# Weights as host-packed blocks with one contiguous 16 KB row per partition, and four token tiles loaded behind the third weight block

## The reference, cut to what matters

```
h = rms_norm(x, norm_mix);  z = h @ w_in
q, kc, vc, ksl, vsl, kw, vw, g, u = split(z)
x = x + concat(sparse_attention(q, kc, vc, ksl, vsl, kw, vw, g),   # compressed, selected, window branches
               conformer_conv(u)) @ w_out
x = x + memory_cross_attention(rms_norm(x), rms_norm(mem), w_mq, w_mk, w_mv, w_mo)
x = x + (silu(h3 @ w_gate) * (h3 @ w_up)) @ w_down,  h3 = rms_norm(x)
```

## Time and profile before

| | |
|---|---|
| median of 3 runs | 1902.3 us (1901.12 to 1903.95) |
| profiled execution | 1897.38 us, span of the slowest core (core 7) 1896.3 us |
| spans of the 8 cores | 1884.6 to 1896.3 us |
| PE busy | 1730.8 us, 91% of the span |
| DVE, ACT, POOL busy | 756.5, 534.7, 160.2 us |
| POOL's DMA queue (software_dynamic) | 182,224 packets, 111.32 MB, 46.3% of 16 engines |
| SP's DMA queue (hardware_dynamic) | 22,640 packets, 52.93 MB, 8.8% |

### The profile page before, as it was taken

The page is one execution under the profiler, slowest core; times in us unless marked ns, Lnnn a source line. Parts: engine busy times, 40 slices in busy tenths (PEclk is TensorE's granted clock), DMA queues, the critical chain, the costliest instruction groups (busy, mean ns, idle before and its releaser), DMA issues.

```text
span 1896.3 us, 30031 instructions; the slowest of 8 cores (1884.6 to 1896.3 us)
## 1 busy us (share of the span) xinstructions
PE 1730.8 (91%) x10862; PEld 939.1 (50%) x10862; DVE 756.5 (40%) x1521; ACT 534.7 (28%) x920; POOL 160.2 (8%) x150
## 2 busy tenths in 40 slices
PE   2699998999996668997789999999999999999998
PEld 1456645666663326865444444444444444444444
DVE  3343122566575454342652332515233251523325
ACT  2243244778676544122551000000000000000000
POOL 2000100000001231001000001000010100001000
PEclk9899999999998988998999999999999999999999
DMA  9920887234136439659317439093663919366364
GB/s 253 164 89 1 95 84 96 49 51 73 35 47 128 122 73 217 95 67 138 44 24 111 64 45 124 14 129 43 92 86 49 125 14 128 42 92 87 48 89 178
DMA packets 205007, 166.17 MB, mean 88 GB/s; under 512 B 14400, under 2 KB 194240, under 8 KB 200512
## 3 DMA queue, kind: packets, MB, share of 16 engines
q0 software_dynamic: 182224, 111.32, 46.3%
q1 hardware_dynamic: 22640, 52.93, 8.8%
HBM read 258.18 MB, written 8.52 MB: 141 GB/s over the span
## 4 chain that ended last, share of the span: by engine, by line
PE 79%; DMA 7%; DVE 4%; ACT 4%; another core or an unknown queue 3%; issue 2%; POOL 1%; SPq 1%; DVEq 0%; ACTq 0%; POOLq 0%
PE bank L1428 16%; PE pair L1425 15%; PE pair L1508 8%; PE bank L1508 8%; PE pair L564 4%; DMA arena<-sel 4%; PE bank L564 4%; PE bank L1266 3%; PE pair L870 2%; PE bank L849 2%; PE bank L723 2%; PE bank L718 2%; PE pair L1319 2%; PE pair L1266 1%
## 5 line engine op out<-in xcount | busy, mean ns | idle before, releaser
L1428 PE MATMUL bank<-arena 128*128 128x512 bf16 x1408 | 318.7, 379 | 0.0
L1425 PE MATMUL pair<-arena 128*128 128x512 bf16 x1344 | 303.8, 379 | 0.0
L1431 ACT ACTIVATE arena<-pair 128x512 bf16<-128x512 f32 x84 | 50.1, 597 | 806.4 <-PE pair L1425 806.4
L1432 DVE TENSOR_TENSOR arena<-bank,arena 128x512 bf16<-128x512 f32 x88 | 60.8, 691 | 537.9 <-PE pair L1425 411.0
L859 ACT ACTIVATE arena<-bank,arena 128x512 bf16<-128x512 f32 (+3 forms) x402 | 215.4, 574 | 75.7 <-PE pair L870 30.9
L1428 PEld LDWEIGHTS bank<-arena 128*128 128x128 bf16 x1408 | 137.6, 98 | 165.4
L1425 PEld LDWEIGHTS pair<-arena 128*128 128x128 bf16 x1344 | 131.6, 98 | 158.5
L1508 PE MATMUL bank<-arena 128*128 128x512 bf16 x704 | 166.3, 379 | 0.0
L1508 PE MATMUL pair<-arena 128*128 128x512 bf16 x704 | 166.3, 379 | 0.0
L870 PE MATMUL pair<-arena 128*128 128x129 bf16 (+1 forms) x1184 | 125.3, 226 | 18.4 <-DVE arena L863 14.7
L1511 DVE TENSOR_TENSOR arena<-pair,arena 128x512 f32<-128x512 f32 x176 | 121.6, 691 | 34.1 <-DVE arena L1511 20.6
(11 more groups left out here) (184 smaller groups left out, 1657.4 us busy)
## 6 DMA issues: line engine op xcount, KB each, us to landing
arena<-xc SPq DMA_DIRECT2D x24, 1024.0 KB, 10.7
arena<-w_gate POOLq DMA_DIRECT2D x22, 1024.0 KB, 14.2
arena<-w_up POOLq DMA_DIRECT2D x22, 1024.0 KB, 15.9
arena<-w_down POOLq DMA_DIRECT2D x22, 1024.0 KB, 12.5
arena<-w_in POOLq DMA_DIRECT2D x18, 1024.0 KB, 13.6
arena<-w_out POOLq DMA_DIRECT2D x10, 1024.0 KB, 18.4
arena<-arena SPq DMA_DIRECT2D x64, 135.0 KB, 2.5
y<-arena SPq DMA_DIRECT2D x8, 1024.0 KB, 3.9
```

Of the source, the lines that this page charges most:

```text
L1425: op(PE, lambda: nc.tensor.matmul(bank[pg][:, :], lhsT=wgt[:, kc, cc * 128:(cc + 1) * 128], rhs=hb[:, kc, :], start=(kc == 0), stop=(kc == ...
L1428: op(PE, lambda: nc.tensor.matmul(bank[pu][:, :], lhsT=wut[:, kc, cc * 128:(cc + 1) * 128], rhs=hb[:, kc, :], start=(kc == 0), stop=(kc == ...
L1432: op(DVE, lambda: nc.vector.tensor_tensor(out=actT[aj][cc][:, tc * 512:(tc + 1) * 512], in0=bank[pu][:, :], in1=sgt[sj][:, :], op=ALU.mult ...
```

## The change

The host packs every weight block into one array, `wblk`, block after block, each as 128 partition rows of 4096 float32 (16 KB); blocks that the ring loads twice are stored once. The device loads block `at` of it into a slot with the same shape as before; the ring's order is the old one. At the start the number of blocks that may be issued is held in `wlimit`: block 0 behind x1, blocks 1 to 3 behind x2, 4 and 5 behind x7. SP waits for block 2's landing before it loads x4, and so x4 to x7. norm_a of tile 4 moves from ahead of the first projection into the middle of the first block, and everything of tiles 4 to 7 moves back by one place, so that norm_b(7) and norm_a(8) stand behind group 0. w_g, w2k and w2v are issued after group 1.

```
-        def wissue(upto=None, behind=None):
+        self.wlimit = 0
+
+        def wissue(limit=None, behind=None):
             POOL.wait(behind)
-            while self.wnext_issue < (len(self.wq) if upto is None else upto):
+            if limit is not None:
+                self.wlimit = limit
+            while self.wnext_issue < self.wlimit:
...
-                dma(POOL, dst, src, w=[wslotb[s_]])
+                dma(POOL, dst, self.wblk_d[at, :, :].rearrange("p (k n) -> p k n", k=shp[0]), w=[wslotb[s_]])
...
         wissue(1, xtok[1])
-        wissue(2, xtok[3])
-        wissue()
-        dma(POOL, wg[:, :, :], self.w_g.rearrange("(k p) n -> p k n", p=128), w=[wgb])
-        dma(POOL, w2[:, 0, :], self.w2k, w=[w2b])
-        dma(POOL, w2[:, 1, :], self.w2v, pw=[w2b])
-
+        wissue(4, xtok[2])
...
             norm_tile_a(xt[xj][:, :], [xtb[xj]], xs0[j], xs0b[j], ss0[j], ss0b[j])
+            if gt == 0:
+                SP.wait(list(wslotb[2].w.values())[0])
             if gt + NX < 16:
-                xload(gt + NX)
+                xtok.append(xload(gt + NX))
+            if gt == 3:
+                wissue(6, xtok[7])
...
+        def late_loads():
+            dma(POOL, wg[:, :, :], self.w_g.rearrange("(k p) n -> p k n", p=128), w=[wgb])
+            dma(POOL, w2[:, 0, :], self.w2k, w=[w2b])
+            dma(POOL, w2[:, 1, :], self.w2v, pw=[w2b])
+
         norm_a(0)
         for gt in range(4):
-            norm_a(gt + 1)
+            if gt < 3:
+                norm_a(gt + 1)
             norm_b(gt)
...
         def next_norm(q_, k_):
-            if q_ < 3 and k_ < 4:
-                gt = (q_ + 1) * 4 + k_
+            gt = (q_ + 1) * 4 + k_
+            if q_ == 0 and k_ < 4:
+                if k_ > 0:
+                    norm_b(gt - 1)
+                norm_a(gt)
+            elif q_ < 3 and k_ < 4:
                 norm_b(gt)
                 if gt + 1 < 16:
                     norm_a(gt + 1)
...
+            if q_ == 0:
+                norm_b(7)
+                norm_a(8)
+                wissue(len(self.wq))
+            if q_ == 1:
+                late_loads()
...
+        out[k] = b.transpose(1, 0, 2).reshape(128, 4096)
```

More of the change, by code:

```diff
@@ L44 @@
 NPTS = 7
+KV_COLS = {"kc": C_KC, "vc": C_VC, "ksl": C_KSL, "vsl": C_VSL, "kw": C_KW, "vw": C_VW}
+BLOCK_ORDER = list(KV_COLS) + [f"q{i}" for i in range(4)] + ["w1k", "w1v"]
+for _i in range(4):
+    BLOCK_ORDER += [f"ua{_i}", f"ub{_i}"]
+BLOCK_ORDER += ["mk0", "mk1", "mv0", "mv1"] + [f"wo{i}" for i in range(8)] + ["mq0", "mq1", "wo1", "wo0", "mq0", "mq1", "mo0", "mo1"]
+BLOCK_ORDER += ["gt0", "up0", "gt1", "up1", "dn0", "dn1"]
+for _i in range(2, 22):
+    BLOCK_ORDER += [f"gt{_i}", f"up{_i}", f"dn{_i}"]
+BLOCKS = list(dict.fromkeys(BLOCK_ORDER))
+BLOCK_AT = {n: i for i, n in enumerate(BLOCKS)}
+NBLK = len(BLOCKS)
 class Sem:
@@ L312, in build @@
         self.memb = dr("memb", [256, D])
-        self.w_in = dr("w_in", [D, IN_W])
         self.w_g = dr("w_g", [D, 24])
[L315 to L324, removed]
+        self.wblk_d = dr("wblk", [NBLK, 128, 4096])
         self.w2k = dr("w2k", [128, 128])
@@ L408, in wissue @@
                     break
-                src, shp = self.wq[i]
+                at, shp = self.wq[i]
                 s_ = i % NSLOT
                 dst = wslot[s_][:, :].rearrange("p (k n) -> p k n", k=shp[0])
-                dma(POOL, dst, src, w=[wslotb[s_]])
+                dma(POOL, dst, self.wblk_d[at, :, :].rearrange("p (k n) -> p k n", k=shp[0]), w=[wslotb[s_]])
                 self.wnext_issue += 1
@@ L448, in wdone @@
             wissue()
[L450 to L488, removed]
+        kvblocks = ["kc", "vc", "ksl", "vsl", "kw", "vw"]
+        for name in BLOCK_ORDER:
+            self.wq.append((BLOCK_AT[name], (32, 128) if name[:2] == "w1" else (2, 2048) if name[:2] in ("mo", "dn") else (16, 256)))
+        self.wo_at = BLOCK_ORDER.index("wo0")
         wg = self.tile(G, "wg", [128, 16, 24], BF16)
@@ L611, in build, with kv_block @@
         kvw = []
-        def kv_block(q_, c0, kind, k_, mid):
+        def kv_block(q_, kind, k_, mid):
             t0_, hb_ = 32 + (q_ % 2) * 512, hTb[q_ % 2]
@@ L656, in build @@
         for q_ in range(4):
-            for k_, (c0, kind) in enumerate(kvblocks):
+            for k_, kind in enumerate(kvblocks):
                 if q_ > 0 or kind not in ("kw", "vw"):
-                    kv_block(q_, c0, kind, k_, lambda: next_norm(q_, k_))
+                    kv_block(q_, kind, k_, lambda: next_norm(q_, k_))
+            if q_ == 0:
[4 more added lines that the diff above has]
+                late_loads()
         S0.close()
@@ L1589, in _pvec, with _pack_blocks @@
     return pv
+def _pack_blocks(I):
+    f = lambda n: np.asarray(I[n], np.float32)[0]
+    w_in, w_out = f("w_in"), f("w_out")[np.concatenate([np.arange(1024), 1024 + CPERM])]
+    cols = lambda w, c: w[:, c:c + 256].reshape(16, 128, 256)
+    rows = lambda w, r: w[r:r + 256].reshape(2, 128, 2048)
+    out = np.empty((NBLK, 128, 4096), np.float32)
+    for n, k in BLOCK_AT.items():
+        if n in KV_COLS:
+            b = cols(w_in, KV_COLS[n])
+        elif n[:2] == "w1":
+            b = f("cmp_k_w1" if n == "w1k" else "cmp_v_w1").reshape(32, 128, 128)
+        else:
+            kind, i = (n[:-1], int(n[-1])) if n[0] == "q" else (n[:2], int(n[2:]))
+            if kind == "q":
+                b = cols(w_in, C_Q + 256 * i)
+            elif kind in ("ua", "ub"):
+                b = cols(w_in, C_U + 256 * i + (1024 if kind == "ub" else 0))
+            elif kind in ("mo", "dn"):
+                b = rows(f({"mo": "w_mo", "dn": "w_down"}[kind]), 256 * i)
+            elif kind == "wo":
+                b = cols(w_out, 256 * i)
+            else:
+                b = cols(f({"mk": "w_mk", "mv": "w_mv", "mq": "w_mq", "gt": "w_gate", "up": "w_up"}[kind]), 256 * i)
+        out[k] = b.transpose(1, 0, 2).reshape(128, 4096)
+    return out
 def make_in_maps(I):
@@ L1596, in make_in_maps @@
     shared = {
[L1597 to L1600, removed]
+        "w_g": np.ascontiguousarray(w_in[:, C_G:C_G + 24]), "wblk": _pack_blocks(I),
+        "w2k": f(I["cmp_k_w2"])[0], "w2v": f(I["cmp_v_w2"])[0],
         "pvec": _pvec(I),
```

## The result

The changed kernel takes 1871.44 us (median of 4 runs, 1871.28 to 1876.15), the kernel before, beside it, 1901.71 (median of 4, 1894.23 to 1903.95). The ratio is 0.9854 with an interval of 0.9822 to 0.9885, so 22 to 34 us less. The forecast was 1874, with 1867 to 1881 for the likeliest case. In the profiled executions the slowest core's span falls from 1896.3 to 1869.9 (26.4), the mean of the eight cores from 1889.5 to 1868.0 (21.5). Some executions run with the cores of one die at a lower granted clock and take some per cent longer; times, ratios and traces here are of the others, and of pieces_4k, which had no other, only the undisturbed die is read.

What follows compares the result with a forecast made beforehand. PE was taken as the bound, with 79% of the chain, and its stops at the start as the main gain. Start 21.2, w_mo 5 and biasT 2 sum to 28.2 us, taking the median from 1902.3 to 1874, range 1857 to 1891.

Steps and rivals of the forecast that it cites:

- the tail before the second group: End of the first projection group: norm_b(7), 8 transposes and two DVE passes hold PE for 3.8 us.
- a stop at x4 in the middle of vc: First projection group: PE stalls 7 us for token tile 4, replacing the old stops.
- block 2 lands at 36: Start: weight blocks land at 24, 30 and 36 us, so SP issues x4 at 36.
- The start: Up to the second projection group: it begins at 75.8 us instead of 96.98, a gain of 21.2 us.
- the bound I named for the forecast: Start: the forecast is wrong if the second projection group begins before 70 or after 82 us.
- the second rival: Weight stream no faster, 8.9 us a block: second group at 84.8, start gains 12 us, 1890 in all; chance 0.2.
- w_mo: PE's waits for the two w_mo blocks: 6 us instead of 10.7, a gain of 5 us, bounds 0 and 12.
- at 5.9 us each: Weight blocks in the new layout: each takes 5.9 us, w_down's 176 GB/s; bounds 8.9 and 4.2 us.
- biasT: ACT's wait for the biasT load, which shares engines with w_in blocks: gain of 2 us, bounds 0 and 5.
- a sign of being wrong: Between 100 and 860 us: a stretch changing length by more than 3 us other than at biasT.
- Weights faster, no stall: First rival: weights at 250 GB/s, PE runs through x4, second group at 66.8, 1858 in all; chance 0.2.
- SP's wait for block 2 turns against it: Third rival: kernel slower; to lose 4 us block 2 must land after 68 us; chance 0.04.

Runs made afterwards that it cites:

- pieces_4k: The changed kernel with each row of a weight block padded into four pieces (4 KB read, 2 KB written); second projection group at 83.14 us on core 0.
- no_wait: The changed kernel without SP's wait for a block before x4; ratio to the kernel before 0.9799 (0.975 to 0.9848).
- after_again: The changed kernel, unaltered, run once more on another chip; ratio to the kernel before 0.9871 (0.985 to 0.9893).
- order_alone: The kernel before with the new order at the start but the old weight layout; ratio to the kernel before 0.992 (0.9893 to 0.9946).
- pieces_short: The changed kernel with block rows padded so pieces can't merge (1 KB read, 512 B written); ratio to the kernel before 0.9907 (0.9881 to 0.9932).
- late_alone: The kernel before with only w_g, w2k and w2v issued later, after group 1; 1891.8 and 1886.1 us, the kernel before on that chip 1899 to 1907.

## Why the prediction was right in the total and wrong in its parts

**What held.** The pieces are merged: 17,616 packets against 17,600 forecast. PE's first projection is at 29.55 (28.7). The memsets no longer wait, the tail before the second group is 3.23 us (3.8 with the norm's passes), and a stop at x4 in the middle of vc takes the place of the old ones. The stretch from 1000 us on has no new wait. The lone rate of a block was sized right: 176 GB/s taken from w_down, 172 measured, though in the FFN short pieces come near it too (163).

**Step that failed: block 2 lands at 36.** It let SP go at 39.87. Two queue rows of the changed kernel, from 20 to 28 us (to be read against the earlier trace rows):

```profile
q0 software_dynamic: 170, 1.26, 91.0%
q1 hardware_dynamic: 77, 0.18, 11.7%
```

Weights flow at 158 GB/s here, above the 133 that I gave them beside x3 and cbf. 0.32 MB had come before 20 us and 1.38 follow until 36, so 2.96 MB at 36 us, where three blocks are 3.15; the queue passes that at 37.3, 1.3 us late. The rest lies in how a block ends. I had put its last byte, counted over the queue, and SP's release on one moment. Two stretches of the changed kernel, from 35.5 to 37.3 and from 37.3 to 39.5 us; the packets under 512 B are the 16 closing packets of block 2:

```profile
DMA packets 40, 0.28 MB, mean 155 GB/s; under 512 B 6, under 2 KB 6, under 8 KB 6
...
DMA packets 56, 0.38 MB, mean 171 GB/s; under 512 B 10, under 2 KB 10, under 8 KB 10
```

Only six of the 16 had come when as many bytes as three blocks hold were through. They run from 35.90 to 39.31, and SP issues 0.6 us after the last: the engines end a block up to 3.4 us apart (2.1 to 3.4 on the eight cores), and those that are through go on with block 3, of which 0.48 MB (3.63 less 3.15) had moved by 40 us. Blocks 0 and 1 were late in the same way, with their last closing packets at 26.2 and 32.3 where I had 24 and 30. The mis-sized term is thus the landing: a block is not there when its bytes, counted over all engines, are through, but when the slowest engine is. x4 then took 8.9 us to its use instead of 8.2, since it shares its way with block 3. Of the 5.5 us by which the second group missed 75.8, 4.7 are these; 0.8 come after x4 (28.3 us from the norm to the second group instead of 27.5).

What x and cast weights do together shows best in no_wait, queues from 28 to 36 us:

```profile
q0 software_dynamic: 115, 0.89, 62.8%
q1 hardware_dynamic: 115, 0.84, 35.6%
```

The packets are equal in number, as the earlier trace rows had it and as the Trainium skill says ("DMA: Bandwidth & Descriptors", Queues, rings and completion order: an engine goes round its queues packet by packet). The page counts several descriptors to a packet, while a packet of these rows is one row or piece; equal counts over 8 us do not tell after how many of them an engine turns. The sum is 1.73 MB in 8 us, 216 GB/s, where I had 266 for the two: a packet of cast weights takes more of an engine's time than an x packet of the same bytes written, 62.8% against 35.6%.

**The start, then, was forecast at 21.2 and gave 15.7** on the slowest cores (96.98 to 81.26), 16.8 by the mark of the start. It stays inside the bound I named for the forecast (second group between 70 and 82), but only just, and after_again, at 82.26, does not. order_alone and pieces_short are what the second rival (stream no faster) looks like: 86.56 and 83.90, against the 84.8 it named, though with lone streams of 139 and 134 GB/s (means of the cores) and not 118.

**w_mo: forecast 5, measured 1 to 2.** The waits are 9.64 us together instead of 6 (10.73 before). The step that failed is "at 5.9 us each". Counted from the issue of the first of the four blocks (862.63 before, 839.75 after), I had them in at 8.0, 15.1, 20.9 and 26.9 us; by their last closing packets they were in at 9.1, 16.9, 23.9 and 30.1, against 9.8, 18.5, 25.0 and 31.6 before. Queue rows of the kernel before, from 872 to 878 us (the second w_mq block, 512 B written a piece) and from 884 to 890 (w_mo, 4 KB):

```profile
q0 software_dynamic: 1547, 0.79, 117.6%
...
q0 software_dynamic: 263, 1.01, 101.7%
```

and of the changed kernel, from 849 to 855 us (the second w_mq block, 8 KB) and from 857 to 863 (w_mo, 8 KB):

```profile
q0 software_dynamic: 117, 0.96, 95.7%
...
q0 software_dynamic: 134, 0.98, 102.5%
```

w_mq went from 132 to 160 GB/s. w_mo, whose pieces were long already, did not gain: 168 before, 163 after. So two of the four blocks could not get shorter, as the lower bound of the forecast had said, and the other two gained less than 118 against 176 had promised: the data of the lone w_in block came mostly from 288 to 296 us, at 131 GB/s, and 118 is what a stretch of 9 us with a start and an end in it gives. Across kernels the stretch with w_mo takes 51.8 to 53.3 us with short pieces (before, order_alone, late_alone, pieces_short) and 48.9 to 50.2 with long ones (the other eight): 2 to 3 us is what length gives there.

**biasT: forecast 2, measured 0.** ACT's wait in the changed kernel, from the view of waits between 280 and 340 us, is 5.6 us against 5.36:

```profile
ACT arena L838 <- DMA arena<-biasT: 5.6, 1, 5.6
```

The lower end of its bounds, 0, was the right one. Why it isn't shorter was not tried.

**Where the total came from.** Sized by the marks: start 16.8, w_mo 2.2, attention and output projection 2.5 (not told from nothing), together 21.5 for the mean core, where 28.2 was forecast. The slowest core's span fell by 26.4: it was 6.8 us above the mean of the eight before and is 1.9 above it after (10.3 in after_again). The median of the runs fell by 30.3, since the profiled execution lay under the median before (1897.4 to 1901.7) and on it after (1871.3 to 1871.4). The slowest core is another one in each profile (7 before, 6 after). From the one to the other POOL's timeline shows 16.9 us at the mark of the start (201.61 to 184.72), 21.1 at the fourth mask of the attention (591.66 to 570.57), 22.9 at the first w_mq block (862.63 to 839.75) and 26.6 at the gate block after w_mo (930.21 to 903.59): 6 us come between the start and w_mq, where I forecast only biasT's 2 and had named 3 us more as a sign of being wrong. In the mean of the eight cores it is 2.4 there. Nothing I ran shows that the change causes the 6 us. The spans of the eight cores lie 7 to 18 us apart in every other kernel of the table, and 3.4 in this profile of the changed one. In after_again, core 1 is 17 us behind core 0 at the end. Waits of its VectorE from 348 to 430 us:

```profile
DVE arena L842 <- POOL arena L922: 7.9, 2, 4.0
```

Core 0 has one such wait there, of 1.6 us. L922 is POOL's multiplication by the mask. So the total was right partly by luck: a miss of 7 us in the steps, by the mean core, was made up by a spread between cores and executions. What sets that spread was not tried and stays open.

**The rivals.** "Weights faster, no stall" (66.8 for the second group) is not what happened: the lone stream at the start moved 172 GB/s and not 250. "SP's wait for block 2 turns against it" did not make the kernel slower, but its mechanism is real and costs about 10 us (81.26 against 71.22); my sum had a stall of 7 us at x4, but of the wait I asked only from which landing on it would turn the change into a loss (68), and not what the change would be without it.

## What to carry to other kernels

When a load is held back so that it won't take bandwidth from another, price the hold itself: here it protected two waits of 0.8 and 1.4 us and cost 10. Here pieces of equal size already gave the two queues an equal share, and the weights hardly needed protection. Look also at what stands behind a load in the issuing engine's own queue: moving three small loads off POOL was worth 14.6 us by itself, more than the new layout alone (5.9 by the same mark). On top of the order with SP's wait the layout gave 5.1 (189.4 to 184.3); what it gives without the wait was not run with short pieces. And a load held until a block lands is held until the slowest engine has it: here that came 2.0 us after the queue had moved as many bytes as the three blocks hold.

## What the runs showed of the hardware that I had not expected

- At the start a stream of weights that are cast on the way moved 172 GB/s written with pieces of 8 KB, 160 with 2 KB and 140 with 512 B: cutting a piece into sixteen costs about a fifth, not the third that 118 against 176 had suggested, and in the FFN next to nothing (165 against 163).
- A piece's length decides its share much more than its speed: with 512 B pieces beside 8 KB packets of x the weights got 0.16 of 2.46 MB in 8 us, with 8 KB pieces 0.89 of 1.73.
- The 16 closing packets of block 2 came 2.1 to 3.4 us apart on the cores of the changed kernel, 1.8 to 3.1 in pieces_short and 3.5 to 4.6 in order_alone, whose pieces lie scattered: the last engine was through later there, though the stream was no slower.
